# A hybrid decoder layer on one core: recurrence preparation merged into its projection, scaling and loads moved

## The reference

```python
mod = silu(c) @ w_mod + b_mod                  # shift1, scale1, gate1, shift2, scale2, gate2
h = rms_norm(x, norm1_g) * (1 + scale1) + shift1
p = h @ w_in
ps = p + mu * (prev - p)                       # the 896 columns of the recurrence; prev is the token before
decay = exp(-exp(-softplus(-(w0 + tanh(wd) @ w_up)) - 0.5))
a, g = sigmoid(a0 + ad @ a_up), sigmoid(gd) @ g_up
kk = heads(k * k_k) * rsqrt(max(sum(kk * kk), 1e-24))
S = S * decay + (S @ -kk) (kk * a) + v k       # per token and head; y = S @ r
m = [(norm(y) + sum(r * k * r_k) * v) * g | gmlp | stick_breaking_attention]
x = x + gate1 * (m @ w_out)
h2 = rms_norm(x, norm2_g) * (1 + scale2) + shift2
x = x + gate2 * hier_moe(h2)                   # best expert group, best 2 of its 4 experts
y = rms_norm(x, final_g)
```

## Time and profile before

| | us |
|---|---|
| three runs, median (lowest, highest) | 1689.82 (1686.15, 1703.18) |
| the profiled execution | 1696.43 |
| its span in the profile | 1694.7 |
| PE busy in the span | 1389.5 |
| DVE, ACT, POOL busy | 633.6, 426.7, 132.1 |

### The profile page before, as it was taken

One profiled execution on the slowest core, in us unless ns is written; L12 is line 12 of the kernel. 1 busy time (PEld: TensorE's weight loads), 2 busy tenths in 40 slices (PEclk: granted clock), 3 DMA queues, 4 the chain that ended last, 5 costly groups with the idle time before them and its releaser, 6 DMA issues. The chain is left out here.

```text
span 1694.7 us, 28956 instructions
## 1 busy us (share of the span) xinstructions
PE 1389.5 (82%) x10623; PEld 802.7 (47%) x10623; DVE 633.6 (37%) x1217; ACT 426.7 (25%) x841; POOL 132.1 (8%) x337
## 2 busy tenths in 40 slices
PE   5999799799999985787666899668992699899946
PEld 2554566444343532554225788524542455555512
DVE  4204222053627183333365455504335122222207
ACT  3101111153637272333331223201111011111113
POOL 0100000010202020000200000030001010000022
PEclk9899799899999997898677899879995799999968
DMA  9102110010101005674550000090001767946755
GB/s 360 44 0 69 27 38 26 26 38 1 38 1 39 1 14 187 211 248 149 200 202 16 16 4 4 4 275 38 29 33 44 267 206 262 352 164 225 258 194 215
DMA packets 87404, 191.64 MB, mean 113 GB/s; under 512 B 17937, under 2 KB 40939, under 8 KB 77709
## 3 DMA queue, kind: packets, MB, share of 16 engines
q1 hardware_dynamic: 73904, 158.09, 26.5%
q0 software_dynamic: 6256, 20.71, 3.6%
q10 hardware_dynamic: 7152, 11.55, 2.2%
HBM read 163.01 MB, written 27.31 MB: 112 GB/s over the span
## 5 line engine op out<-in xcount | busy, mean ns | idle before, releaser
L2492 PE MATMUL ex_ps_g<-ex_w,ex_xt 128*64 128x256 f32 x1344 | 160.1, 393 | 24.0 <-DMA ex_w<-in_exp_wu 22.6
L2186 PE MATMUL op_ps_o<-op_w,op_m_t 128*128 128x512 f32 (+1 forms) x288 | 130.3, 607 | 21.5 <-DMA op_w<-in_w_out 21.5
L2492 PEld LDWEIGHTS ex_ps_g<-ex_w,ex_xt 128*64 128x64 f32 x1344 | 99.0, 141 | 72.7 <-DMA ex_w<-in_exp_wu 15.8
L1587 PE MATMUL at_ps_z<-mix_hT,at_w 128*128 128x363 f32 (+1 forms) x384 | 121.3, 474 | 10.1 <-DMA at_w<-in_w_in 10.1
L463 PE MATMUL rp_ps<-mix_hT,rp_w 128*128 128x363 f32 (+1 forms) x336 | 106.1, 478 | 8.0 <-DMA rp_w<-in_w_in 8.0
L1736 DVE TENSOR_SCALAR at_zc<-at_ps_z,at_bias 128x512 f32<-128x512 f32 (+3 forms) x96 | 54.5, 613 | 141.8 <-PE at_ps_z L1603 141.0
L1587 PEld LDWEIGHTS at_ps_z<-mix_hT,at_w 128*128 128x128 f32 x384 | 73.1, 192 | 56.9 <-DMA at_w<-in_w_in 10.3
L338 PE MATMUL fr_big<-all_mT,mix_hT 128*128 128x256 f32 (+3 forms) x288 | 95.0, 493 | 3.1 <-DVE mix_hT L391 3.1
L2186 PEld LDWEIGHTS op_ps_o<-op_w,op_m_t 128*128 128x128 f32 (+1 forms) x288 | 53.2, 189 | 87.6 <-issue 85.4
L2509 PE MATMUL ex_ps_y<-ex_wd,ex_hid_T 128*64 128x512 f32 x336 | 82.3, 610 | 13.0 <-DMA ex_wd<-in_exp_wd 11.8
L463 PEld LDWEIGHTS rp_ps<-mix_hT,rp_w 128*128 128x128 f32 x336 | 64.9, 194 | 47.9 <-DMA rp_w<-in_w_in 8.3
(11 more groups left out here) (473 smaller groups left out, 2079.9 us busy)
## 6 DMA issues: line engine op xcount, KB each, us to landing
ex_w<-in_exp_wg SPq DMA_DIRECT2D x17, 1024.0 KB, 4.9
ex_w<-in_exp_wu SPq DMA_DIRECT2D x17, 1024.0 KB, 8.0
ex_wd<-in_exp_wd SPq DMA_DIRECT2D x17, 1024.0 KB, 7.6
sa_k<-in_cache_k SPq DMA_DIRECT2D x64, 256.0 KB, 4.1
sa_v<-in_cache_v SPq DMA_DIRECT2D x64, 256.0 KB, 5.0
rq_w_mod<-in_w_mod SPq DMA_DIRECT2D x16, 1024.0 KB, 7.1
slot_rows<-ex_y ACTq DMA_DIRECT2D x84, 128.0 KB, 5.6
fr_w<-in_w_mod SPq DMA_DIRECT2D x8, 1024.0 KB, 10.8
```

The costliest lines, as they stand in the source:

```text
L1587: last = nc.tensor.matmul(third(x_, c), w[:, x_, k, :], hT[:, k, lo:hi], start=(k == 0), stop=(k == KT - 1))
L2186: last = nc.tensor.matmul(ps_o[0:m, u, lo:lo + 512], m_t[:, u, k, 0:m], w[:, k, lo:lo + 512], start=(k == 0), stop=(k == KT - 1))
L2492: final = nc.tensor.matmul(ps_g[rows, u, 0:DE], xt[:, k, HALVES[u]], w1[:, u, x_, k, :], start=(k == 0), stop=(k == KT - 1))
```

## The change

1. `rwkv_prepare` is gone as a phase; its work is done inside `rwkv_project`. The rows come in the order LoRA, k0, r0, k1, r1, v0, v1, in pieces of 384, 384 and 320 tokens, into three PSUM slots. Between the pieces PE runs the ups, head sums, gates and bonus sums by a hand-written table and the 16 modulation steps by `mods_at`. The modulation has two buffers (one lies in `v_g`, still free then), one PSUM bank and one kept sum; the bias comes as four rows. ACT and DVE have tables of the same kind.
2. `B` has two parts instead of four: the end-scaled keys are not made. The state is added first and scaled afterwards. The bonus stands in `mT`, y in `R`.
3. Attention's first weights are loaded into `v_g` at the end of the merged phase; the last-token stores are waited for at the end of attention.
4. In sampled attention the keys' pages lie in `hT`, `q_all` is gone, POOL stages the queries with two copies, and several tiles share memory.
5. `w_out` is loaded into `hT` during `rwkv_chunks`. The order of SP's list in `out_project` changes, x comes in two loads, and the `gate2` and `final` loads move there from `experts`.
6. In `experts` `w1` lies in `mT`, `wd` in `hT`; the last `wd` load stands ahead of the zero stores. `combine` gathers into `mT` and `hT`. The front's weight ring and `x_own` lie in `B` and `rwkv_g`.

In the first block below, the first loop is SP's, `project`, `between` and the second loop are PE's; then comes a line of ACT's table, whose entries run ahead of the copy `keep_p(n, c)`, and DVE's table, whose entries run ahead of `mix(n, c)`. n counts rows in the new order, c pieces. `keys(f)` holds the reciprocal, `logs` the scan, `products` the rest of the preparation for f.

```diff
+    LORA, PIECES, SLOTS = 6, ((0, 384), (384, 768), (768, TOK)), 3
+    ORDER = (LORA, 2, 0, 3, 1, 4, 5)
+    mods_at = {(n, c): 1 for n in range(2, RF) for c in range(3)}
+    for at in ((2, 0), (2, 1), (6, 1), (6, 2)):
+        mods_at.pop(at)
+    for at in ((3, 2), (4, 2), (5, 2), (5, 0), (4, 1)):
+        mods_at[at] = 2
...
+                for n in range(RF):
+                    for c in range(3):
+                        for i in range(mods_before[n, c], mods_before[n, c] + mods_at.get((n, c), 0)):
+                            sp.wait_ge(s["mod_step"], i + 1)
+                            if i % KT == 0 and i // KT + 1 < WIDES:
+                                load_bias(i // KT + 1)
+                            if i + 2 < MOD_STEPS:
+                                load_mod_step(i + 2)
+                            elif i % 2 == 0:
+                                for x_ in range(2):
+                                    at = OQ + x_ * SBW
+                                    sp.dma_start(keep["at_w"][:, x_, :, :], w_view[:, :, at:at + P]).then_inc(keep["at_w_loaded"], 16)
+                        if (n, c) == (4, 2):
+                            store_lasts(0, range(0, FIRST_LASTS))
+                        if (n, c) == after_wide[0]:
+                            store_mod(0)
+                    if n + 2 < RF:
+                        sp.wait_ge(s["projected"], 3 * (n + 1))
+                        load(n + 2)
+                store_mod(1)
+                store_lasts(1, range(FIRST_LASTS, RF))
+                sp.wait_ge(s["mod_stored"], WIDES * QUADS * 16)
...
+                def project(n, c):
+                    i, (lo, hi) = 3 * n + c, PIECES[c]
+                    if c == 0:
+                        pe.wait_ge(w_loaded[n % 2], n // 2 * 16 + 16)
+                    if i >= SLOTS:
+                        pe.wait_ge(s["p_kept"], i - SLOTS + 1)
...
+                between = {(0, 1): turn_carried,
+                           (1, 1): lambda: ups((0, 0), (0, 1)),
+                           (1, 2): lambda: ups((0, 2), (1, 0)),
+                           (2, 0): lambda: ups((1, 1), (1, 2)),
+                           (2, 1): lambda: head_sums(0),
+                           (3, 0): lambda: gate_ups(0),
+                           (3, 1): lambda: gate_ups(1),
+                           (4, 0): lambda: head_sums(1),
+                           (4, 1): lambda: turn_lasts(range(0, FIRST_LASTS)),
+                           (5, 1): lambda: bonus_sums(0),
+                           (6, 1): lambda: bonus_sums(1)}
+                for n in range(RF):
+                    for c in range(3):
+                        project(n, c)
+                        if (n, c) in between:
+                            between[n, c]()
+                        for i in range(mods_before[n, c], mods_before[n, c] + mods_at.get((n, c), 0)):
+                            modulate(i)
+                turn_lasts(range(FIRST_LASTS, RF))
...
+                          (4, 0): lambda: square(1),
...
+                before = {(1, 2): lambda: (logs(0, 0), logs(0, 1)),
+                          (2, 0): lambda: (logs(0, 2), logs(1, 0)),
+                          (2, 1): lambda: (logs(1, 1), logs(1, 2)),
+                          (3, 0): lambda: keys(0),
+                          (3, 1): lambda: products(0),
+                          (4, 2): lambda: keys(1),
+                          (5, 1): lambda: products(1),
+                          (6, 0): lambda: [bonus(0, c) for c in range(3)]}
```

```diff
-                    for f in range(2):
-                        last = V.scalar_tensor_tensor(S[:, 1 - ch, f, :], S[:, ch, f, :], ends[:, f, at:at + 1],
-                                                      ones(3)[:, f, :], ALU.mult, ALU.add)
+                    V.tensor_tensor(S_sum[:, :, :], S[:, ch, :, :], ones(3)[:, 0:2, :], ALU.add).then_inc(g["S_added"], 1)
+                    dve.wait_ge(g["S_added"], at + 1)
+                    V.tensor_tensor(S[:, 1 - ch, :, :], S_sum[:, :, :], bc(ends[:, :, at], 2, C), ALU.mult).then_inc(g["s_kept"], 1)
```

```diff
                 load_mod(sp, gate["p"], mod_rows, 2, s["gate_loaded"])
+                sp.dma_start(x1[:, 0:2, :], x_tiles[:, 0:2, :]).then_inc(x_loaded[0], 16)
                 load_mod(sp, gain["p"], mod_rows, 4, s["mod_loaded"])
                 load_mod(sp, shift["p"], mod_rows, 3, s["mod_loaded"])
...
+                sp.dma_start(x1[:, 2:NT, :], x_tiles[:, 2:NT, :]).then_inc(x_loaded[1], 16)
+                sp.dma_start(x1[0:NS, NT, :], T["x_sample"]).then_inc(x_loaded[1], 16)
+                load_mod(sp, keep["gate2"]["p"], mod_rows, 5, keep["gate2_loaded"])
+                load_mod_sampled(sp, keep["gate2"]["s"], mod_rows, 5, keep["gate2_loaded"])
+                sp.dma_start(keep["final"][:, :], T["final_g"].to_broadcast([P, D])).then_inc(keep["gate2_loaded"], 16)
```

More of the change, by code:

```diff
@@ L711, in _ @@
+                for n in range(RF):
+                    for c in range(3):
+                        if (n, c) in before:
+                            before[n, c]()
+                        keep_p(n, c)
+                        if (n, c) == after_wide[0]:
+                            keep_mod(0)
+                    if n == 0:
+                        keep_carried()
+                    keep_lasts(n)
+                keep_mod(1)
+                keep_rows(1, FIRST_LASTS, RF)
             @block.vector
@@ new lines, in _ @@
+                for n in range(RF):
+                    for c in range(3):
+                        if (n, c) in before:
+                            before[n, c]()
+                        mix(n, c)
+                        if n == RF - 1:
+                            if c == 2:
+                                bonus(1, 0)
+                                bonus(1, 1)
+                                bonus(1, 2)
+CONSTS = 5
+DONE = {(0, "kk"): 3, (0, "prod"): 8, (1, "kk"): 16, (1, "prod"): 21}
@@ L772, in rwkv_chunks @@
 def rwkv_chunks(nc, T, keep):
-    gates, bonus = keep["rwkv_g"], keep["bonus"]
+    gates = keep["rwkv_g"]
     R, B, mT, ends = keep["R"], keep["B"], keep["mT"], keep["ends"]
```

714 lines of the change are left out of this document (360 added, 354 removed).

## The result

The changed kernel takes 1590.63 us (median of 4 runs, 1588.56 to 1593.40), the kernel before 1692.57 (1686.15 to 1703.18): a ratio of 0.9393, with a 95% interval of 0.9339 to 0.9447. That is 102 us, where 86 were forecast (1604 as a median), inside the range of 1572 to 1642. The profiled execution of the changed kernel took 1593.40 us, its span is 1591.7.

The account below looks back on a forecast made before the run. PE, busy for 82% of the span, was taken as the bound. Terms -49.9 + 1 - 6.8 - 2 - 19 - 6 - 3 sum to -85.7: 1610.7 us profiled, 1604 as a median; range 1572 to 1642.

Parts of the forecast that it names:

- rival (b): Whole kernel: no stall, overlapping ups, costless end and state update, more from the last wd; 1588 as a median; chance 0.10.
- the stalls: Merged phase: PE waits for modulation loads, some 6 of them late, taken at 6 us (bounds 0 to 28).
- the last wd: End of experts: load issued ahead of the zero stores, -3 us (bounds -9 to -1); the larger gain had 9.
- the ups and the end: Merged phase: LoRA ups at 5.6 us and a 1.5 us longer end; overlapping ups and a costless end would save 3.5.
- The merge: Preparation moved into the projection: 93.5 us go, the projection grows by 43.6 (bounds 34 to 72), net -49.9.
- The cover: Merged phase: about 3 us of slack before head_sums(1) waits for square(1); beyond it each DVE microsecond delays PE by one.
- rival (a): Whole kernel, half of the gain: 14 loads late by 2 us, out_project's norm still held; 1637 as a median; chance 0.20.
- out_project: Output weights loaded during the chunks: products end and the first turn comes at 1133, -19 us; other end some -8.
- Experts: Experts phase: ten loads moved out of the first round, -6 us, and the last wd load issued earlier, -3.
- Sampled attention: Sampled attention's start: a memset and eight copies leave the chain before PE's first product, -2 us (bounds -2.7 to 0).
- Chunks: Chunks' state update: addition then dependent multiplication, 16 updates each perhaps 0.06 us longer, +1 us (bounds 0 to 2.5).
- The rule: Merged phase: 34 tiling-mode changes drain TensorE by the skill; priced at nothing, or 5 us more (1609) by the rule.

Follow-up runs that it names:

- the 10.5 us of DVE work: Changed kernel with twelve more DVE operations of 0.84 us (a repeated product, same result) in keys(0): 1598.07 us.
- the version that should beat both: Changed kernel with first projection weights loaded earlier, modulation and last-row stores moved later, second modulation sum kept earlier, zero stores in the first expert round: 1588.81 us.
- the serial version: Changed kernel with all projection pieces first, then preparation and modulation in the same order, in the same phase: 1633.96 us.

## Why the prediction was right

The sign, the order of the terms and the place of each were right; of the 15.6 us that it fell short, these are the terms that were mis-sized. Nearly all of them erred to the same side, so that 1590.63 lies nearer to rival (b), *a larger gain*, at 1588 than to the forecast of 1604. Of (b)'s reasons the stalls gave 3.4 of its 6 us, the last wd 4 of 6, the ups and the end 1.6 of 3.5.

*The merge.* Forecast +43.6 for the projection, measured +39 (154.7 and 153.4 against 115.2 and 114.5). PE's work grew by 35.0 us (36.1 forecast; the LoRA ups took 4.3 and not 5.6), the end by 1.3 (1.5 forecast). The step that was off is "I take 6 us" of stalls: they are 2.6. The landing times were taken from a phase with four loads under way, where the median was 7.1 us and not 5.7. (The table `mods_at` has eleven slots, five of them with two steps, not twelve and four; the sum of 16 steps is the same.) Two buffers were enough with pieces of 5.3 us between; with one the waits are 25 us. That the preparation is hidden by PE's own work, rather than merely removed, is shown by the run without interleaving, which gives back 46 of the 54 us. Of these 54, 21 are PE's own work, which took 163.6 us in two phases and takes 142.4 at the higher clock; the rest is idle time.

*The cover.* "About 3 us of slack" at square(1) was 4.0, and it decides as it was argued: the 10.5 us of DVE work pushed PE by 6.4. What the prediction missed is that such a wait costs PE more than its own length, through the clock: 2.9 us more here. For rival (a), whose 14 loads come 2 us late each, that stays open: waits of 4.9 us, in the run with one buffer, were followed by slow work, waits of 1.0 and 1.4 us by steps of 1.07 (the timeline of the version that should beat both), and no run of the interleaved phase has waits of 2 us.

*out_project.* -19 came from the turn at 32 us after the start: it came at 31.5 instead of 51.0. The phase won 22. The other 2 to 3 us are slow work that went with the first stall: the first turn and the product behind it took 9.97 us (1152.03 to 1162.00) and now take 7.74 (1065.10 to 1072.84). The loads ahead of the first norm took 19.7 us, not the 11 that were worked out by bytes at the pace of the earlier burst: SP's issue of the last router weights, 8.0 us of it, was not in that sum. The norm was still ready in time, with 4 us to spare.

*Experts.* -9 was forecast and about -14 measured. The loads of gate2 were sized rightly: the wait of 7.3 us is now 0.6, 6.7 less for 6 forecast. The order of the last wd was worth 7 and not 3. The step that failed is "the loop still has to end, and it now starts after that load": it does, but the loop and the last product then run beside each other, where before they stood in a row.

*Attention* was right to half a microsecond. *Sampled attention*: the first turn of keys comes 20.9 instead of 23.7 us after the phase's start, the 2.7 us of the two rows; the rest, 1 us by the mean of the twelve profiles, is not told apart from the spread of that phase. *Chunks*: +1.8 for a forecast of +1, but not for the reason given: the two-step update costs nothing that the runs show, and for the load beside it they show no cost either. Of the 1.8, 1.1 to 1.3 us lie ahead of the first update, where the granted clock differs between runs; what sets it stays open.

*The rule.* The prediction set the price of a change of tiling mode at none, because rows began before the end of the one ahead. That reading was wrong: ends of matmuls are modelled, and from start to start a change costs about 0.10 us. The Trainium skill, page TensorEngine Tiling (Array Packing), section Tiling Modes, says that TensorE drains there; the trace agrees in that each change costs time, and the page has no price. It did no harm to the sum: some 32 such changes are about 3 of the phase's 142 us of PE work, by this estimate, and that work came out 1.1 us under the forecast.

## What to carry to other kernels

A serial phase whose engines wait for each other is worth hiding in a phase that keeps PE busy, as long as the chain's last link into PE has slack; look for that link in the hand-written order and price a miss with the clock, not with the wait alone. When loads are moved early, ask what the engine behind the first consumer waits for as well: here the weights and the order of the rest would each have brought only 12 and 8 of the 22 us alone. Landing times went with the number of loads under way (medians of 7.1, 5.7 and 4.8 us with four, two and one), so they are not to be carried over from a deeper ring.

## What the runs showed that was not expected

A wait on PE was paid twice. After 6.4 us of idle time PE ran at 0.50 of full speed, the 1.2 GHz level, for 5.8 us; in the serial version 35 us of work took 58 at a mean of 0.64; with one buffer 13 of 36 us were slower work. The Trainium skill, page TensorE: Matmul & The Clock Gate, section HAM oscillation — how this bites in real kernels, tells of waits for DMA that leave the next work at the lower clock; the run with one buffer agrees (a step of 1.93 us instead of 1.06 after a wait of 4.89, and 0.89 over the phase). And a phase that the change doesn't touch, gated_mlp, lasted 44.3 to 49.0 us in the profiles of both kernels, while sampled attention varied by 7 us and the experts by 6 where nothing in them was edited: differences of whole phases below that, in one profile each, are no evidence.
